# Forgetting attention run as one sequence of 64 units with v as the stationary operand, banded attention with q loaded earlier and other engine orders

## The reference: two blocks over one sequence of 1024 tokens

```
def forgetting_attention(q, k, v, f_logit):          # first block: 8 heads of 64, 1024 tokens
    c = cumsum(log_sigmoid(f_logit))                  # one decay row per head
    for each block i of 128 queries:
        s = q_i @ k.T * scale + c_i[:, None] - c[None, :]
        s = where(kpos <= qpos, s, -inf)              # causal: i + 1 key tiles of 128 count
        out_i = softmax(s) @ v

def window_gqa_mixer(...):                            # second block: 16 query heads, 4 key heads
    keys = 256 context keys and the tokens within +-128
    p = softmax over [context, band, sink logit of the head]
    out = (p @ v) * silu(gate)
```

## Time and profile before

| what | us |
|---|---|
| median of 3 runs | 3324.4 (3321.92 to 3340.68) |
| the profiled execution: its own time | 3323.97 |
| its span | 3322.2 |
| PE busy, share of the span | 2993.3 (90%) |
| DVE / ACT / POOL busy | 1736.5 / 983.0 / 1051.4 |
| forgetting attention, last product before it to first of w_out | 387.06 to 595.69 |
| banded attention, first score to last weighted sum | about 2919 to 3206 |

### The profile page before, as it was taken

How to read it: one execution, slowest core, us unless ns; L and a number is a source line. 1 busy time by engine, 2 the same in 40 slices (tenths; PEclk the granted TensorE clock), 3 DMA queues, 4 the chain that set the end, 5 groups by cost and what they waited for, 6 DMA issues and landing times. The chain is left out here.

```text
span 3322.2 us, 44046 instructions
## 1 busy us (share of the span) xinstructions
PE 2993.3 (90%) x16336; PEld 2471.0 (74%) x16336; DVE 1736.5 (52%) x2469; ACT 983.0 (30%) x1703; POOL 1051.4 (32%) x641
## 2 busy tenths in 40 slices
PE   3789978999999999989999997889889698889998
PEld 2578767777777777768777887878778477767776
DVE  5644334375554545455557337878743552056753
ACT  2112234231111111131101206767641200166731
POOL 1523300374435544433222221222233432201122
PEclk6899988999999999989999999999999799999999
DMA  2454332111111111013336312121111132242111
GB/s 83 146 162 135 108 90 57 44 51 51 51 38 44 54 47 44 25 45 107 120 115 202 130 59 104 70 75 49 56 34 38 32 120 88 82 127 53 33 39 64
DMA packets 213037, 255.03 MB, mean 77 GB/s; under 512 B 9193, under 2 KB 181518, under 8 KB 212894
## 3 DMA queue, kind: packets, MB, share of 16 engines
q1 hardware_dynamic: 197318, 189.68, 19.1%
q10 hardware_dynamic: 15584, 63.51, 4.8%
HBM read 187.56 MB, written 65.60 MB: 76 GB/s over the span
## 5 line engine op out<-in xcount | busy, mean ns | idle before, releaser
L913 PE MATMUL ps<-hh,w_parts 128*128 128x512 f32 (+2 forms) x2560 | 1002.7, 392 | 76.1 <-POOL hl L743 32.6
L914 PE MATMUL ps<-hl,w_parts 128*128 128x512 f32 (+2 forms) x2560 | 985.7, 385 | 0.0
L915 PE MATMUL ps<-hh,w_parts 128*128 128x512 f32 (+2 forms) x2560 | 983.5, 384 | 0.0
L704 POOL TENSOR_TENSOR w_parts<-w_raw,zero 128x1024 fp32r<-128x1024 f32 x140 | 288.8, 2063 | 1165.4 <-PE ps L915 818.7
L913 PEld LDWEIGHTS ps<-hh,w_parts 128*128 128x128 f32 x2560 | 489.7, 191 | 193.3 <-issue 65.3
L914 PEld LDWEIGHTS ps<-hl,w_parts 128*128 128x128 f32 x2560 | 492.1, 192 | 105.1 <-issue 5.7
L915 PEld LDWEIGHTS ps<-hh,w_parts 128*128 128x128 f32 x2560 | 490.3, 192 | 100.1
L706 POOL TENSOR_TENSOR w_parts<-w_raw,w_parts 128x1024 fp32r<-128x1024 f32 x140 | 339.5, 2425 | 11.0
L1783 ACT ACTIVATE f_y<-f_z,convv 128x1024 f32<-128x1024 f32 x44 | 54.8, 1245 | 532.6 <-DVE f_z L2342 532.5
L2518 DVE TENSOR_SCALAR_CACHE_REDUCE b_s<-ps 128x640 f32<-128x640 f32 (+1 forms) x128 | 101.3, 792 | 194.2 <-PE ps L1439 118.1
L913 PE MATMUL ps<-f_hi,d_hi 128*128 128x512 f32 x352 | 139.6, 396 | 20.1 <-DVE res L2379 14.1
(11 more groups left out here) (323 smaller groups left out, 4952.6 us busy)
## 6 DMA issues: line engine op xcount, KB each, us to landing
w_mod_sb<-in_w_mod SPq DMA_DIRECT2D x16, 1536.0 KB, 7.1
w_raw<-in_w_up SPq DMA_DIRECT2D x44, 512.0 KB, 3.7
w_raw<-in_a_w_in SPq DMA_DIRECT2D x32, 512.0 KB, 4.1
d_raw<-in_w_down SPq DMA_DIRECT2D x22, 512.0 KB, 4.1
w_raw<-in_w_in SPq DMA_DIRECT2D x20, 512.0 KB, 4.8
za_parts<-z_hi ACTq DMA_DIRECT2D x16, 640.0 KB, 3.0
za_parts<-z_lo ACTq DMA_DIRECT2D x16, 640.0 KB, 4.1
d_even<-za_parts SPq DMA_DIRECT2D x16, 640.0 KB, 7.0
```

The lines of the kernel that those rows point to most:

```text
L704: pool.tensor_tensor(wh[:, s], w_raw[:, s], zero[:].broadcast_to([P, KT * P]), ALU.add).then_inc(w_high[s], 1)
L913: pe.matmul(out_, w_hi, x_hi, start=start, stop=False)
L914: pe.matmul(out_, w_hi, x_lo, start=False, stop=False)
L915: return pe.matmul(out_, w_lo, x_hi, start=False, stop=stop)
```

## The change

Forgetting attention is one sequence of 64 units, written out without a loop over pairs. Unit u has pair j = u // 16, block i and head a, the two heads of a block in turn. Scores run 3 units ahead (`FA_LEAD`).
- Loads: the keys have two places (`a_k1[0]`, `a_k1[1]`; the low part of odd pairs lies in the context columns of `hl`), `a_q2` has two (`wl`, `wh`), and the stacked q of pair j lies in rows 4 + j of `hh` and `hl`. Pair 1 is loaded right behind pair 0, pairs 2 and 3 as soon as pair 0 and pair 1 are scored. v is transposed for pair j + 1 at units 12 and 14 of pair j.
- Product with v: v is the stationary operand in two column halves of 64, one per head, and 128 columns of probabilities move; it is issued for both heads of a block together, and the result comes out in the layout of `hh`.
- The sums: the transposes of `a_o` go. Every 2 blocks PE spreads the reciprocals (`fa_spread`, 4 products), ACT copies them (`fa_keep_rows`), DVE multiplies (`fa_output`), ACT makes the high part (`fa_keep_high`) and POOL the low part.
- POOL's split of the first w_out tile moves between the last low parts, that of the second behind them.

Banded attention: SyncE's wait for the last stored gate ahead of the q loads goes (the one ahead of the gate loads stays). ACT takes 3 exponentials ahead instead of 4. DVE copies unit u before it takes the maximum of unit u + 4, and takes the reciprocals after both. A semaphore is merged into `ba.low`.

```diff
-            def fa_load(j):
-                for to, part, row in ((a_q1[0:DH], 0, 0), (a_q1[DH:P], 1, 0), (a_k1[0:DH], 0, 4), (a_k1[DH:P], 0, 4), (a_k2[0:DH], 1, 4)):
...
+            def fa_load_q(j):
+                sp.dma_start(a_q2[j % 2][0:DH].bitcast(F32), z1_parts[0, j * P:(j + 1) * P, :].rearrange("(a p) n -> p a n", p=DH)).then_inc(
+                    fa_loaded[j % 2], 16)
+                for a, to in enumerate((hh, hl)):
+                    for part in range(2):
+                        sp.dma_start(to[part * DH:(part + 1) * DH, 4 + j, X_COLS].bitcast(F32),
+                                     z1_parts[part, j * P + a * DH:j * P + (a + 1) * DH, :]).then_inc(fa_loaded[j % 2], 16)
...
-            fa_load(0)
+            fa_load_k(0)
+            fa_load_v(0)
+            for s in range(2):
+                sp.wait_ge(w_used[s], W0["w_out"][s] + 1)
+            fa_load_q(0)
             for s in range(2):
                 sp.wait_ge(stored[s], 16 * (Z0["vb"][s] + 2) + 16)
-            with sp.Fori(1, 4) as j:
-                sp.wait_ge(fa.scored, 16 * j + 1)
-                fa_load(j)
+            fa_load_q(1)
+            fa_load_v(1)
+            fa_load_k(1)
+            for j in (2, 3):
+                sp.wait_ge(fa.scored, 2 * QB * (j - 1))
+                fa_load_q(j)
+                fa_load_k(j)
+                fa_load_v(j)
...
-            for s in range(2):
-                sp.wait_ge(stored[s], 16 * (Z0["b_gate"][s] + 4) + 16)
+
             def ba_load_q(h, c):
...
+            def fa_mix(b):
+                j, i = divmod(b, QB)
+                g, t = b // 2, b % 2
+                for u in (2 * b, 2 * b + 1):
+                    for n in range(len(fa_batches(i))):
+                        z, before = fa_turn("p", u, n)
+                        pe.wait_ge(fa_copied[z], before + 1)
+                if t == 0 and g >= 2:
+                    pe.wait_ge(fa.normed, fa_outputs(g - 2))
                 for kt in range(i + 1):
-                    last = pe.matmul(got, a_pt[:, u % 2, kt], a_v[:, kt, a * DH:(a + 1) * DH], start=(kt == 0), stop=(kt == i))
+                    for a in range(2):
+                        last = pe.matmul(bank(6 + g % 2)[a * DH:(a + 1) * DH, t * P:(t + 1) * P],
+                                         a_v[j % 2][:, kt // 2, kt % 2 * P + a * DH:kt % 2 * P + (a + 1) * DH], a_pt[:, (2 * b + a) % FA_LEAD, kt],
+                                         start=(kt == 0), stop=(kt == i))
...
+            for u in range(FA_UNITS + 1):
+                if u + FA_LEAD < FA_UNITS:
+                    fa_scores(u + FA_LEAD)
+                if u < FA_UNITS:
+                    j, i, a = fa_unit(u)
+                    pe.wait_ge(fa.exped, u + 1)
+                    for n, blocks in enumerate(fa_batches(i)):
+                        fa_turn_tiles(lambda kt: a_s[:, u % FA_LEAD, kt * P:(kt + 1) * P], blocks, "p", u, n)
+                    if u % (2 * QB) in (12, 14) and u < 6 * QB:
+                        fa_turn_v(j + 1, u % (2 * QB) // 2 - 6)
+                if u % 2 == 0 and u >= 2:
+                    fa_mix(u // 2 - 1)
+                if u % 4 == 0 and u >= 4:
+                    fa_spread(u // 4 - 1)
+            pe.wait_ge(fa.low, FA_UNITS // 4)
...
-            for u in range(BA_LEAD):
+            for u in range(BA_LEAD - 1):
                 ba_exp(u)
...
             for u in range(BA_UNITS + 6):
                 if u < BA_UNITS:
+                    ba_copy(u)
+                    if u + BA_LEAD < BA_UNITS:
+                        ba_max(u + BA_LEAD)
                     if u % 4 == 1:
                         ba_norm(u // 4)
-                    if u + BA_LEAD < BA_UNITS:
-                        ba_max(u + BA_LEAD)
-                    ba_copy(u)
```

More of the change, by code:

```diff
@@ L100, in fa_batches, with fa_unit, fa_plan, fa_turn @@
     return batches(i + 1)
[L103 to L121, removed]
+FA_UNITS = 4 * QB * 2
+FA_LEAD = 3
+def fa_unit(u):
+    j, n = divmod(u, 2 * QB)
+    return j, n // 2, n % 2
+def fa_plan():
+    turns = [("v", 0, n) for n in range(2)]
+    for u in range(FA_UNITS):
+        turns += [("p", u, n) for n in range(len(fa_batches(fa_unit(u)[1])))]
+        if u % (2 * QB) in (12, 14) and u < 6 * QB:
+            turns.append(("v", u // (2 * QB) + 1, u % (2 * QB) // 2 - 6))
+    return {key: divmod(n, 2)[::-1] for n, key in enumerate(turns)}
+def fa_turn(*key):
+    return fa_plan()[key]
+def fa_mixes(b):
+    return b + b // 2 + 1
+def fa_spreads(g):
+    return 3 * g + 3
+def fa_norms(g):
+    return max(2 * g, 1)
+def fa_outputs(g):
+    return 2 * g + 3 if g < 4 * QB // 2 - 1 else 2 * g + 2
 def band_tiles(i):
@@ L1249, in _, with fa_spread @@
-            fa_pair(0, True)
-            with pe.Fori(1, 4) as j:
-                fa_pair(j, False)
-            fa_turn_output(4)
-            for n in range(2):
-                b, before = fa_turn(4, "o", n)
-                pe.wait_ge(fa_free[b], before + 1 + 1)
+            def fa_spread(g):
+                pe.wait_ge(fa.normed, fa_norms(g))
+                for t in range(2):
+                    for a in range(2):
+                        n = 2 * t + a
+                        last = pe.matmul(bank(6 + g % 2)[a * DH:(a + 1) * DH, (2 + t) * P:(3 + t) * P],
+                                         a_rec[:, g % 2, n:n + 1].broadcast_to([P, DH]), ident[:], start=True, stop=True)
+                last.then_inc(fa.mixed, 1)
@@ L1487, in _ @@
                         ba_mix(u // 4 - 1, n)
-            pe.wait_ge(ba.low, 32)
+            pe.wait_ge(ba.low, 64)
             OUT_BANKS = ((6, 7), (2, 5))
@@ L2306, in _, with fa_copy @@
-            for u in range(LEAD):
-                fa_max(0, u)
+            def fa_copy(u):
+                for n, blocks in enumerate(fa_batches(fa_unit(u)[1])):
+                    b, before = fa_turn("p", u, n)
+                    if b == 1:
+                        dve.wait_ge(fa_turned[b], before + 1)
+                        if u >= FA_LEAD:
+                            dve.wait_ge(fa.mixed, fa_mixes((u - FA_LEAD) // 2))
+                        dve.tensor_copy(a_pt[:, u % FA_LEAD, blocks.start:blocks.stop, :],
+                                        bank(4 + b)[:, 0:len(blocks) * P].rearrange("p (k q) -> p k q", q=P)).then_inc(fa_copied[b], 1)
```

351 lines of the change are left out of this document (188 added, 163 removed).

## The result

The change takes 94 us off. The kernel after has a median of 3229.96 us (3226.04 to 3231.9, 4 runs), the kernel before beside it 3323.88 (3321.92 to 3340.68, 4 runs); the ratio is 0.9708, 95% interval 0.9681 to 0.9735. Forecast were 3239 us, with 3211 to 3264 as the range. The profiled execution took 3229.67 us, its span 3228.0.

What follows compares the result with a forecast made beforehand. PE was taken to bound both attentions, apart from its waits for loads between pairs and ahead of banded attention's first score. Forgetting attention -60.4 and banded -24.1 make -84.5, from 3323.97 to 3239 us; range 3211 to 3264.

Steps and rivals of the forecast that it cites:

- Loads, -33.2: Forgetting attention, between pairs: q, k and v loaded earlier, so three load waits of PE go, -33.2 us.
- Slow starts, -10.2: Forgetting attention, after each load wait: low clock and empty pipeline go, less 1 us per pair given back, -10.2 us.
- The start, +4.5: Start of forgetting attention: four more DMAs, 1.05 MB, stand behind the last use of the weights, +4.5 us.
- The product with v, -22.5: Forgetting attention: passes in column halves 0.055 us apart instead of 0.109, with switching costs, new spreads, no output transposes, -22.5 us.
- halves don't run together: Rival, product with v: pitch stays 0.109 us, this term becomes +8.6 instead of -22.5, total 3270 us; chance 0.08.
- ACT and DVE extras, 0: Forgetting attention: ACT's two more copies and DVE's one more product per 2 blocks are hidden by PE, 0 us.
- hand-overs bound PE: Rival, forgetting attention: PE waits in 40 of 64 units, 0.4 us each, +16 us, total 3255; chance 0.14.
- Banded start, -18.1: Start of banded attention: earlier q and k loads, ACT earlier with a shorter lead, less a clock loss, -18.1 us.
- 20.1 us earlier: Start of banded attention: ACT starts when the gates are stored, 2901.35 instead of 2921.41, 20.1 us earlier.
- +3 for the clock: Start of banded attention: PE waits in pieces and may run its first units at clock 0.50, +3 us.
- Banded body, -6: Body of banded attention: DVE's copy ahead of the maximum removes PE's waits for it, -6 us, bounds 0 and -12.
- No effect on unchanged code: Code outside the two attentions, including the middle from `w_out` to the gate projection: forecast change 0 us.

## Why the prediction was right, and where not

The total was missed by 9 us because two errors partly cancelled: forgetting attention gave 6.4 less than forecast and the unchanged middle, for which I forecast nothing, 16.5 more. That the middle helped is luck. Without it the time would have been about 3246, which the stated range also holds, so the range doesn't owe its hit to it.

1. *Loads, -33.2: right.* The three waits are gone, pair 1's too. Holding the loads back brought waits of 49.1 us.
2. *Slow starts, -10.2: the size is borne out, its derivation was wrong.* I took pair 1's two windows for the same tiles plus 16 transposes. They aren't, since the products trail the scores. These are the product rows of the first window, then of the second:

```profile
L1220 PE MATMUL ps<-a_v,a_pt 128*128 128x64 f32 x56 | 7.6, 282 | 0.0
L1220 PE MATMUL ps<-a_v,a_pt 128*128 128x64 f32 x88 | 10.7, 270 | 0.0
```

The first has 32 passes fewer and 13 products of scores and masks more, so the 4.4 us a start were read from unequal work. Copies of both kernels on one chip have stages of 210.8 and 153.2, so -57.6. Taking off -33.2, +5.8 (start), -22.5, +1 and +4.3 (step 5, below) leaves -13.0; from the first pair of profiles, with +6.1 and a difference of -54.0, it is -9.7. The bounds were -13 and -6. The loads held back give an estimate of 11 that doesn't need this balance. No run isolates the term.
3. *The start, +4.5: too small.* It is +6.1, outside my bound of +6 by a little. PE waited for the last of pair 0's five q DMAs, issued by 392.7. The 1.05 MB more are 4.9 us at the window's 216 GB/s; what makes up the rest no run isolates. With q asked for in two parts it is +0.8.
4. *The product with v, -22.5: mechanism right.* The pitch is 0.055, as taken over from the spread. Counted in both traces from each start on PE to the next, without pauses over 1 us, the products fell from 61.8 to 35.2 us and the output's transposes (5.8) went; the transposes of probabilities grew from 33.6 to 38.6, and the spreads are 9.1. Together this is -18.3, and -22.5 with the 4.3 that step 5 left out is -18.2. The rival "halves don't run together" (3270) is out. "TensorE: Matmul & The Clock Gate" of the Trainium skill, in the part on packing small matmuls, lets a weight load overlap only for another row group, and on issuing says that matmuls stay in program order. The first did not hold here (0.055 with both halves in the same rows). Against the second stand the starts at 477.60 to 477.87 of the run with the heads' products apart, where spreads begin ahead of products that precede them in the program.
5. *ACT and DVE extras, 0: the step of this stage that failed.* I compared busy shares (ACT and DVE at half of PE's time) and took it that nothing would wait. But the transposes of v stand in PE's order ahead of the products, and PE stood there for banks that ACT and DVE were still copying, at each pair's end. Moved behind the products they cost 4.3 us less (153.2 to 148.9; 4.2 to 5.9 against kernels on the same chip). This is the rival "hand-overs bound PE" on a small scale: it was priced at 16 us for 40 units, and happened at three places. What is left of the 6.4 us is the start (1.6) and the rest of the balance in step 2 (0.5).
6. *Banded start, -18.1: measured -16.2*, from 34.7 to 18.5 us at unit 8's mask product; the load wait alone is 14.9 of it. The term that was off is "20.1 us earlier" for ACT: I took the store's landing from before, 2.7 us after its issue, and the moved loads made it 6.9. That is 4.2 of loss. The new orders gave 1.3 with the old wait in place (34.7 before, 33.4), but nothing with the loads early (18.1 with the old orders, 18.1 to 18.5 without). So of the +3 for the clock the balance leaves 0 to 1 (20.1 - 4.2 - 16.2, and 1.3 more). The second unit's transposes came 12.9 us after the first score, where I had said 8.
7. *Banded body, -6: measured -8.6 to -8.9*, within the bounds; the price left out PE's own waits. The units behind the body give another 0.9, which I had at nothing.
8. *No effect on unchanged code: wrong, and by 16.5 us the largest miss.* In the middle the time at the lower clock fell from 136.1 to 109.2 us, of which differential attention has 34.1 to 13.7; the copies show it again. At 0.45 us each, these 26.9 us are 12 of the 16.5. What in the change brings the clock up is open: the loads held back, with all else new, also brought a middle of 2293.2, which speaks for the pauses in forgetting attention; the kernel with the v transposes moved has 2292.7 without them, which speaks against. That 8 products more took 11 to 14 us from differential attention in the kernel before suggests that where short pauses fall decides; that they left the changed kernel where it was is not explained by it. Either way I see no row of before from which this could have been priced.

## What to carry to other kernels

Give column halves alternating products in the code: the pitch of two interleaved halves was half that of one, and PE made up for the wrong order over four passes only. When a long product sequence is joined and loads are pulled ahead, ask of each small block of transposes whose PSUM bank it needs and put it behind the products that need none; shares of busy time say nothing on that. Ask of a load that is pulled ahead which store it will meet, and who waits for that store. Split the first load of a stage so that its first unit can start, and judge such edits by the stage's length in the trace, since the rest of the kernel moves by 10 us and more with its time at the lower clock.

## What was new about the hardware

PE started matmuls out of the order of the program when they went to the other column half, up to four passes ahead. And a stage whose engines all do the same work took 426.4 to 439.9 us, with 6.8 to 34.1 us of it at the lower of the two granted clocks (0.50 of full speed). In the kernel before, eight superfluous products were enough to move it from one end to the other; in the changed kernel they left it at 427.3.
